# A hybrid decoder step on one core: where the refills, the last sums and the fourth quad's weights stand in the down products

## The reference

```
x = x + 0.5 * swiglu(rmsnorm(x, g_ffn1), w1_gate, w1_up, w1_down)
h = rmsnorm(x, g_mix) @ w_in          # RG-LRU heads | sliding-window attention heads
x = x + concat([lru_out, attn_out]) @ w_out
x = x + cross_attend(rmsnorm(x, g_xattn), memory keys, memory values)
x = x + 0.5 * swiglu(rmsnorm(x, g_ffn2), w2_gate, w2_up, w2_down)
y = rmsnorm(x, g_final)
swiglu(x) = (silu(x @ w_gate) * (x @ w_up)) @ w_down
```

## Time and profile before

| | |
|---|---|
| median of 3 runs | 2235.63 us (2232.41 to 2236.86) |
| the profiled execution's own time | 2234.07 us |
| its span | 2232.2 us |
| TensorE (PE) busy | 2128.1 us, 95% |
| VectorE (DVE) busy | 1595.1 us, 71% |
| ScalarE (ACT) busy | 772.9 us, 35% |
| GpSimd (POOL) busy | 514.1 us, 23% |
| DMA | 271.94 MB, 122 GB/s on average |

### The profile page before, as it was taken

One profiled execution on the slowest core, in us unless ns is written; L12 is line 12 of the kernel. 1 busy time (PEld: TensorE's weight loads), 2 busy tenths in 40 slices (PEclk: granted clock), 3 DMA queues, 4 the chain that ended last, 5 costly groups with the idle time before them and its releaser, 6 DMA issues. The chain is left out here.

```text
span 2232.2 us, 39480 instructions
## 1 busy us (share of the span) xinstructions
PE 2128.1 (95%) x15452; PEld 2013.8 (90%) x15452; DVE 1595.1 (71%) x2295; ACT 772.9 (35%) x1360; POOL 514.1 (23%) x499
## 2 busy tenths in 40 slices
PE   6899999999899999989999999998999999998998
PEld 5899999999898888877898887988999999998987
DVE  7877877878579578899526155368778778775884
ACT  6423323333233224557403034154233233322332
POOL 1011111101000256778635321520121121010002
PEclk9999999999999999999999999999999999999999
DMA  3223333255634121153411062312233233556332
GB/s 139 76 95 131 114 125 131 105 187 199 232 112 166 68 113 38 63 150 95 165 38 58 19 245 77 134 39 77 94 131 135 104 131 127 190 201 253 112 121 81
DMA packets 82296, 271.94 MB, mean 122 GB/s; under 512 B 9095, under 2 KB 21383, under 8 KB 68615
## 3 DMA queue, kind: packets, MB, share of 16 engines
q1 hardware_dynamic: 79232, 267.01, 32.6%
q10 hardware_dynamic: 2951, 3.35, 0.4%
HBM read 191.22 MB, written 76.32 MB: 120 GB/s over the span
## 5 line engine op out<-in xcount | busy, mean ns | idle before, releaser
L914 PE MATMUL ps<-act_hi,op_hi 128*128 128x272 f32 x1712 | 496.0, 290 | 31.2 <-DVE u L2321 22.7
L915 PE MATMUL ps<-act_lo,op_hi 128*128 128x272 f32 x1712 | 496.3, 290 | 0.0
L916 PE MATMUL ps<-act_hi,op_lo 128*128 128x272 f32 x1712 | 495.6, 289 | 0.0
L914 PE MATMUL ps<-t_hi,op_hi 128*128 128x272 f32 x1392 | 403.5, 290 | 7.3 <-DVE op_lo L2148 7.1
L916 PE MATMUL ps<-t_hi,op_lo 128*128 128x272 f32 x1392 | 403.0, 290 | 0.0
L915 PE MATMUL ps<-t_lo,op_hi 128*128 128x272 f32 x1392 | 402.8, 289 | 0.0
L914 PEld LDWEIGHTS ps<-act_hi,op_hi 128*128 128x128 f32 x1712 | 325.4, 190 | 34.5 <-issue 32.6
L1599 ACT ACTIVATE op_hi<-sums 128x512 fp32r<-128x512 f32 (+2 forms) x232 | 138.9, 599 | 548.9 <-DVE sums L2154 330.7
L822 POOL TENSOR_TENSOR hid_o<-hid_o 128x544 f32<-128x544 f32 x72 | 113.9, 1582 | 921.0 <-DMA hid<-hid_o 916.8
L915 PEld LDWEIGHTS ps<-act_lo,op_hi 128*128 128x128 f32 x1712 | 324.9, 190 | 0.0
L916 PEld LDWEIGHTS ps<-act_hi,op_lo 128*128 128x128 f32 x1712 | 324.5, 190 | 0.0
(11 more groups left out here) (354 smaller groups left out, 3952.1 us busy)
## 6 DMA issues: line engine op xcount, KB each, us to landing
raw_gu<-in_w_gu SPq DMA_DIRECT2D x40, 1024.0 KB, 6.8
w_raw<-in_w_plain SPq DMA_DIRECT2D x54, 512.0 KB, 3.3
hid<-hid_o SPq DMA_DIRECT2D x20, 1088.0 KB, 4.9
hid_t<-hid_o SPq DMA_DIRECT2D x18, 1088.0 KB, 4.0
hid_h<-sum_hi SPq DMA_DIRECT2D x16, 544.0 KB, 5.2
x<-x_keep SPq DMA_DIRECT2D x16, 544.0 KB, 6.2
raw_dq<-in_w_dq SPq DMA_DIRECT2D x8, 1024.0 KB, 7.8
ck_T<-in_ck SPq DMA_DIRECT2D x8, 1024.0 KB, 6.7
```

Of the source, the lines that this page charges most:

```text
L914: pe.matmul(out, wh, ah, start=(first and n == 0), stop=False, skip_group_check=goes_on)
L915: pe.matmul(out, wh, al, start=False, stop=False, skip_group_check=goes_on)
L916: ins = pe.matmul(out, wl, ah, start=False, stop=end, skip_group_check=goes_on)
```

## The change

Four edits. (1) SPLIT_OPS is (3, 4): operand 5 is stored raw, one high-part tile and one store less for each pair, and it is refilled on ACT and DVE like operand 6. (2) In a quad that opens a group, ACT makes the high parts of operands 5 and 6 after steps 1 and 2, and the next quad's weight parts 0 to 2 behind them; DVE makes the low part of operand 5 after C11, and the sums for the next quad after the low part of operand 6 instead of at the quad's start. (3) On SP, operand 6 of group 0 goes out ahead of the second row of x. (4) On SP, the weights of quad QUADS + 3 go out right behind those of QUADS + 2, ahead of the store of the last sums.

```diff
--- before.py
+++ after.py
@@ -82,10 +82,10 @@
 LAST_K = [2 * p + i for p in LAST_PAIRS for i in range(2)]
 LAST_ROWS = (2, 3, 6, 7)
 assert sorted([p for p0, kh in DOWN_GROUPS for p in range(p0, p0 + kh)] + [PAIR_AT.index(p) for p in LAST_PAIRS]) == list(range(FI))
-SPLIT_OPS = (3, 4, 5)
-RAW_OPS = (0, 1, 2, 6)
+SPLIT_OPS = (3, 4)
+RAW_OPS = (0, 1, 2, 5, 6)
 SUMMED = FI - 2
-OUTS = 3
+OUTS = 2
 SWAPS = 4
 QK = GRP + 1
 HALF_HEADS = NH // 2
@@ -250,11 +250,8 @@
         u3 = at("u3", [P, 2, TQ], X0 + KH * ROW + 2 * ROW)
         tmp = at("tmp", [P, 2, 2, TQ], X0 + KH * ROW + 2 * ROW + 4 * TH)
         hid_o = at("hid_o", [P, 2, T], X0)
-        sum_off = (X0 + 2 * ROW, X0 + KH * ROW + 3 * ROW + 4 * TH)
-        sum_hi = [at(f"sum_hi{i}", [P, 1, w], sum_off[i], F32R) for i, w in enumerate((T, TH))]
-        assert X0 + KH * ROW + 2 * ROW + 4 * TH + ROW <= sum_off[1] and sum_off[1] + 4 * TH <= A0
-        end_off = (X0 + KH * ROW + 2 * ROW + 4 * TH, X0 + KH * ROW + 2 * ROW)
-        end_hi = [at(f"end_hi{i}", [P, 1, w], end_off[i], F32R) for i, w in enumerate((T, TH))]
+        sum_hi = at("sum_hi", [P, 1, T], X0 + 2 * ROW, F32R)
+        end_hi = at("end_hi", [P, 1, T], X0 + KH * ROW + 2 * ROW + 4 * TH, F32R)
 
         def half(row, h):
             return row[:, h * TH:(h + 1) * TH].rearrange("p (a n) -> p a n", a=2)
@@ -450,7 +447,7 @@
                        hid_f=2 * NC + 4 * (FI - 1), hid_out=16 * (FI + 1), xg=KT, t_sum=8, t_hi=8, t_lo=8,
                        w_sum=4 * ALL_QUADS, w_hi=STEPS * ALL_QUADS, w_lo=STEPS * ALL_QUADS, quad_mm=STEPS * ALL_QUADS,
                        quad_ev=EVICTS * ALL_QUADS, p1_kept=ALL_QUADS, scaled=3 * QUADS // 2, up_own=3 * QUADS // 2,
-                       sum_hi=2 * SUMMED, sum_lo=2 * SUMMED, t_made=4 * SUMMED, t_out=16 * OUTS * SUMMED, x_added=3 * DOWN_QUADS,
+                       sum_hi=SUMMED, sum_lo=SUMMED, t_made=4 * SUMMED, t_out=16 * OUTS * SUMMED, x_added=3 * DOWN_QUADS,
                        mv_hi=len(RAW_OPS) * len(DOWN_GROUPS), mv_lo=len(RAW_OPS) * len(DOWN_GROUPS),
                        last_in=16 * (4 + 2 * NC), last_hi=4 + NC, last_lo=4 + NC, dn_mm=NC * KT, dn_ev=NC * KT)
         MV_IN = [sum(32 if j in SPLIT_OPS else 16 for j in range(i, STEPS, 3)) for i in range(3)]
@@ -596,9 +593,8 @@
                              hid_o[:, :, :].rearrange("p m n -> p (m n)")).then_inc(f["t_out"], 16)
 
             def store_highs(f, i, high=sum_hi):
-                sp.dma_start(t_in["hid_h"][:, i, 0:2, :].rearrange("p a n -> p (a n)"), high[0][:, 0, :].bitcast(F32))\
+                sp.dma_start(t_in["hid_h"][:, i, :, :].rearrange("p a n -> p (a n)"), high[:, 0, :].bitcast(F32))\
                   .then_inc(f["t_out"], 16)
-                sp.dma_start(t_in["hid_h"][:, i, 2, :], high[1][:, 0, :].bitcast(F32)).then_inc(f["t_out"], 16)
 
             def store_hidden(f, i, v):
                 sp.wait_ge(f["hid_f"], v)
@@ -624,7 +620,7 @@
                     store_hidden(f, i, i * 4 + upto(f, "hid_f", 2 * NC))
                     sp.wait_ge(f["w_lo"], i * (2 * STEPS) + upto(f, "w_lo", STEPS))
                     load_quad(f, w, i * 2 + 4, 0)
-                    store_sums(f, i, i * 2 + upto(f, "sum_lo", 0))
+                    store_sums(f, i, i + upto(f, "sum_lo", 0))
                     store_highs(f, i)
                 sp.wait_ge(f["w_lo"], upto(f, "w_lo", SUMMED * (2 * STEPS)))
                 load_quad(f, w, SUMMED * 2 + 3, 1)
@@ -640,23 +636,23 @@
                 sp.wait_ge(f["t_out"], upto(f, "t_out", 16 * OUTS * (SUMMED - 1)))
                 x_again(1, 0)
                 load_down(f, dq, QUADS + 1)
-                load_moving(f, 0, range(6))
-                sp.wait_ge(f["quad_mm"], upto(f, "quad_mm", STEPS * QUADS))
+                load_moving(f, 0)
                 sp.wait_ge(*x_back_again(f, 1, 1))
                 x_again(1, 1)
-                load_moving(f, 0, range(6, 7))
                 store_hidden(f, PAIR_AT.index(FI - 1), upto(f, "hid_f", 2 * NC + 4 * (FI - 1)))
                 for m in range(2):
                     x_again(2, m)
                 load_down(f, dq, QUADS + 2)
-                store_sums(f, PAIR_AT.index(FI - 1), upto(f, "sum_lo", 2 * SUMMED))
+                load_down(f, dq, QUADS + 3)
+                store_sums(f, PAIR_AT.index(FI - 1), upto(f, "sum_lo", SUMMED))
                 store_highs(f, PAIR_AT.index(FI - 1), end_hi)
                 sp.wait_ge(f["t_out"], upto(f, "t_out", 16 * OUTS * SUMMED))
                 for q in (3, 0):
                     for m in range(2):
                         x_again(q, m)
                 for n in range(QUADS + 3, ALL_QUADS):
-                    load_down(f, dq, n)
+                    if n > QUADS + 3:
+                        load_down(f, dq, n)
                     u = Quad(n - 2)
                     if u.ends_before_group():
                         load_moving(f, u.group() + 1)
@@ -1611,8 +1607,7 @@
 
                 made = 4 * SUMMED if u.down() else 0
                 act.wait_ge(f["t_made"], upto(f, "t_made", made) if made else u.turn(4, upto(f, "t_made", 0)))
-                act.activation(high[0][:, :, :], hid_o[:, 0:1, :], ACT.Copy).then_inc(f["sum_hi"], 1)
-                act.activation(high[1][:, :, :], hid_o[:, 1:2, 0:TH], ACT.Copy).then_inc(f["sum_hi"], 1)
+                act.activation(high[:, :, :], hid_o[:, 0:1, :], ACT.Copy).then_inc(f["sum_hi"], 1)
 
             def keep_p1(f, u):
                 act.wait_ge(f["quad_mm"], u.count(STEPS, upto(f, "quad_mm", 1)))
@@ -1636,8 +1631,8 @@
                     act.wait_ge(f["quad_mm"], u.count(STEPS, upto(f, "quad_mm", j + 1)))
                     if j == 0 and u.later():
                         keep_p1(f, u)
-                    if u.opens_group() and j == 3:
-                        refill_hi(f, u.group(), 6)
+                    if u.opens_group() and j in (1, 2):
+                        refill_hi(f, u.group(), 4 + j)
                     if u.opens_down() and j == 0:
                         quad_hi(f, u, s, STEPS - 1)
                     gate = s == 0 and not u.down()
@@ -1645,7 +1640,10 @@
                         quad_silu(f, u, 0)
                     if gate and j >= 5:
                         quad_silu(f, u, j - 4)
-                    if prepare and not (n.opens_down() and j == STEPS - 1):
+                    if u.opens_group() and j == 2:
+                        for v in range(3):
+                            quad_hi(f, n, 1 - s, v)
+                    elif prepare and not (u.opens_group() and j < 2) and not (n.opens_down() and j == STEPS - 1):
                         quad_hi(f, n, 1 - s, j)
                     if gate and j == 4 and u.i is not None:
                         sums_hi(f, u)
@@ -2266,11 +2264,10 @@
 
             def sums_lo(f, u, high=sum_hi):
 
-                for i, part in enumerate((hid_o[:, 0:1, :], hid_o[:, 1:2, 0:TH])):
-                    made = 2 * (SUMMED - 1) + i + 1 if u.down() else 0
-                    dve.wait_ge(f["sum_hi"], upto(f, "sum_hi", made) if made else u.turn(2, upto(f, "sum_hi", i - 1)))
-                    dve.tensor_tensor(part.bitcast(F32R), part, high[i][:, :, :].bitcast(F32), ALU.subtract)\
-                       .then_inc(f["sum_lo"], 1)
+                dve.wait_ge(f["sum_hi"], upto(f, "sum_hi", SUMMED) if u.down() else u.turn(1, upto(f, "sum_hi", 0)))
+                part = hid_o[:, 0:1, :]
+                dve.tensor_tensor(part.bitcast(F32R), part, high[:, :, :].bitcast(F32), ALU.subtract)\
+                   .then_inc(f["sum_lo"], 1)
 
             def refill_lo(f, g, j):
                 hi, lo, raw = operand(j, DOWN_GROUPS[g][1])
@@ -2321,13 +2318,10 @@
                     return dve.scalar_tensor_tensor(out=to[:, :, :], in0=ps[:, 2:4, 0:TQ], scalar=0.5, in1=p1[:, :, :],
                                                     op0=ALU.mult, op1=ALU.add).then_inc(f["quad_ev"], 1)
 
-                def last_low():
+                if not u.opens_down():
                     quad_lo(f, u, s, 6)
-                    if prepare:
-                        quad_sums(f, n, 1 - s)
-
-                if not u.opens_down():
-                    last_low()
+                if not u.opens_group() and prepare:
+                    quad_sums(f, n, 1 - s)
                 made(1)
                 dve.wait_ge(f["p1_kept"], u.count(1, upto(f, "p1_kept", 1)))
                 dve.wait_ge(f["quad_ev"], u.count(EVICTS, upto(f, "quad_ev", 0)))
@@ -2343,7 +2337,9 @@
                 made(2)
                 add_bank(0, 0, 0)
                 if u.opens_down():
-                    last_low()
+                    quad_lo(f, u, s, 6)
+                if u.opens_group():
+                    refill_lo(f, g, 5)
                 if not u.opens_group():
                     low(1)
                 if final:
```

## The result

| | kernel before | changed kernel |
|---|---|---|
| median | 2236.24 us (2232.41 to 2237.94, 4 runs) | 2203.31 us (2202.47 to 2212.15, 4 runs) |
| ratio | | 0.9864, interval 0.9836 to 0.9892 |
| profiled execution, span | 2234.07, 2232.2 | 2212.15, 2210.3 |
| TensorE, DVE busy | 2128.1, 1595.1 | 2127.8, 1593.4 |
| DMA | 271.94 MB | 261.91 MB |

The account below looks back on a forecast made before the run. TensorE, busy nearly throughout, was taken as the bound, with waits chiefly from a late-issued weight load. Terms 21.8 + 3.8 - 0.4 + 2.8 = 28.0 us took 2234.07 to 2206.1; median forecast 2208 us, range 2203 to 2212.

Parts of the forecast that it names:

- The load: Fourth down quad's weights, issued earlier, end TensorE's long waits and the low clock behind them: 21.8 us over both layers.
- rival E: Fourth down quad: the weight load isn't earlier, since the low copies hold it; 2235 us, chance 0.02.
- x as the next wait: First layer: x rows behind the last sums' store land at 569.1, delaying eviction C22; 0.5 us lost, nothing in the second.
- Rival B: First layer: x rows land 4 us or more later than taken and become the new wait; 2216 us, chance 0.07.
- Group 0: Down group 0's opening: operand 6 lands 4.2 us earlier, DVE's chain to p1 becomes 1.9 us earlier; 3.8 us, two layers.
- Step 5 waits for operand 5: Sign of being wrong: TensorE's step 5 waits for operand 5, where only 0.2 to 0.3 us was expected lost.
- The GpSimd term: Group 0's opening: GpSimd's four hidden-pair sums make four DVE instructions 1.15 us longer each, 4.6 us, unchanged by the edits.
- Locking: DVE and GpSimd's shared ports lock per instruction: four DVE instructions slowed; if all six, 2 x 1.15 us more a layer.
- rival C: Group openings gain in full, 6 us a layer, as weight sums slip ahead or GpSimd's come later; 2200 us, chance 0.11.
- rival A: Clock falls again where group 0 opens, after several short waits, 3.4 us per fall; 2215 us, chance 0.15.
- Groups 1 and 2: Later down groups: group 1 -0.4 us over both layers; group 2 1.4 us each from earlier QUADS+10 weights, 2.8 together.
- The loop: Quad loop: nine times one ACT copy, DVE copy and 272 KB store less, TensorE without gap; value 0, bounds 0 and 1.

Follow-up runs that it names:

- load_only: Kernel before with only the fourth down quad's weight load issued ahead of the store of the last sums; 2212.29 us, ratio 0.9894.
- three_split: Changed kernel's orders with operand 5 still stored split, so three operands split as before; 2211.78 us, ratio 0.9894 to the kernel before.
- x_swapped: Changed kernel with the x rows of q=0 issued ahead of those of q=3; 2210.3 us, ratio 0.9888 to the kernel before.
- after_again: Changed kernel unchanged, run and profiled a second time; 2205.31 us, ratio 0.9868 to the kernel before.
- pool_late: Changed kernel with GpSimd's last four hidden-pair sums held until p1 of quad QUADS+1 is kept; 2199.28 us, ratio 0.9842 to the kernel before.
- after_w10: Changed kernel with the weights of QUADS + 10 issued ahead of the last operands; 2205.53 us, ratio 0.9876 to the kernel before.
- sums_early: Changed kernel with the next quad's two weight sums back at the start of a group's opening quad; 2204.17 us, ratio 0.9859 to the kernel before.
- rest_only: Changed kernel without the moved weight load, which again stands behind the store of the last sums; 2224.04 us, ratio 0.9953 to the kernel before.
- before_again: Kernel before, unchanged, profiled a second time; 2237.53 us, span 2234.7.
- sums_pool: Changed kernel with the edits of both sums_early and pool_late; 2197.05 us, ratio 0.9832 to the kernel before.
- best_w10: sums_pool with the weights of QUADS + 10 issued ahead of the last operands; 2194.96 us, ratio 0.9831 to the kernel before.

## Why the prediction was right, step by step

**The load.** Right in cause and size, along the chain of the earlier trace rows. The terms were 21.8 us; edit (4) alone gave 21.7 by the medians, and 11.0 and 9.7 in the two group-0 stretches (12.2 and 9.6 forecast; the 1.7 us at C22, put at 0.5, are the difference in the first). The waits fell to nothing and the two low-clock stretches behind them went (rival E is out). The first term was read from one profile: the second profile of before has 9.2 us in that place and not 10.7.

**x as the next wait.** Rightly named, mis-sized in the end on the safe side. x was put at 569.1 with 0.5 us lost; it came at 564.90 with none. The four loads went out 2.8 us earlier than before (559.57), as the 1.3 us of the shorter store and group 0's shift give, and DVE had its row 5.3 us after that. With a third store in front the time was 7.8 us (load_only, 562.64 to 570.44) and 7.1 (three_split). In the seven profiles with two stores and the same order of x rows and weights it is 5.3 to 6.6, five of them below 6. So the third store goes with 0.5 to 2.5 us; by what means no run shows. In layer 2 it is 5.1 to 5.4 with three stores or two. Rival B's condition never came, and x_swapped shows what it costs near its edge. DVE stood 3.08 and 3.89 us at x; TensorE, whose idle stretch the sign of being wrong must mean (DVE's own was forecast), did not wait there.

**Group 0.** The landings were forecast at 516.2 and 519.0 and came at 517.0 and 519.7, DVE's low copy of operand 6 at 522.66 for 522.1. TensorE then waited 1.2 us for operand 5, not 0.2 to 0.3: DVE was waiting for ACT's t_hi, which waited for the transfer, so 0.8 us of landing went straight into that wait. "Step 5 waits for operand 5" was one of the prediction's signs of being wrong, and in this one opening it came. It was one late landing: in after_again the same copy started at 516.0 and the wait was 0.2, as forecast, and in layer 2 neither profile has one. Counted from the first refill, p1 was 1.4 us sooner than before in this opening and 2.3 to 2.7 in the other three, where 1.9 was claimed. The GpSimd term held: four DVE instructions at 1.74 to 1.84 us, the fifth at 0.68, and pool_late priced it at 3.9 to 4.3 us a layer. Locking was the better count than sharing: the number is GpSimd's four. The Trainium skill (SBUF — State Buffer, "SBUF: two separate sides") has it so for instructions with two SBUF inputs; the eviction of U2 in pool_late, with one of its inputs in PSUM, took 0.71 us beside GpSimd and agrees. That rival C's 8 us could be had was right too, but it took an edit: pool_late.

**The clock (rival A).** In layer 1 the fall did come, in both profiles (0.93 over 520:545; before had 0.86); in layer 2 the clock stayed up (1.00 over 1960:1990, 205 matmuls) where before it had been 0.83 over 1970:1990. What failed of A is its price. The fall stands ahead of p1, and there DVE's chain sets the pace and not TensorE. after_w10 has the same code and no fall in this opening:

```profile
520.00:545.00 25.00, 22.34 (x160) 21.56 (x159) 24.12 (x30) 8.68 (x14) 7.80 (x4) 0.93 0.35 134
...
520.00:545.00 25.00, 20.84 (x161) 20.05 (x160) 24.12 (x30) 8.65 (x14) 7.79 (x4) 1.00 0.35 136
```

The first row is after_again's, the second after_w10's. p1 is kept at 536.64 and 536.59, and group 0 takes 89.48 and 89.46 us. Without the fall TensorE only waits longer for p1, 1.5 us; with it, not at all. In layer 2 it is the other way round, after_w10 with the fall and the changed kernel without: 89.21 against 89.17 and 89.18. So a fall under this chain costs nothing, where A had put 3.4 us; in sums_early, behind p1, it does cost. Whether the clock falls is less settled. The Trainium skill (TensorE: Matmul & The Clock Gate, "A second HAM failure mode: psum-queue depth-cycling") holds that pauses, when frequent enough, make it swing. Ten openings here have the same wait of 1.9 us among shorter ones (after, after_again, rest_only, x_swapped, after_w10); five show the fall and five don't. What decides between them no run shows.

**Groups 1 and 2.** The cost of the moved sums in group 1 was put too low. Where the sums stand at the quad's start it takes 69.13 to 69.16 us, in nine of twelve openings of before, before_again, load_only, sums_early, sums_pool and best_w10; where they were moved, 69.81 to 69.84 in all fourteen. The moved sums thus cost 0.7 us in each layer, 1.3 together, where 0 and 0.4 had been claimed; TensorE waits 0.4 to 0.5 us for p1 there. The first profile of before hides it in layer 1, because operand 6 came late in it (a wait of 1.7 us, 1.1 in the second), and the 71.47 of before_again turns it into a gain in layer 2. Group 2's 1.4 us came in layer 1 (DVE's wait 3.21 to 0.69). The step that failed is its second half: in layer 2 the gain of the means is 0.5 and not 1.4, and against the first profile of before it is a loss of 0.3 to 0.7. DVE's wait and SP's last issues there:

```profile
2115.46 0.43 DVE L2137 TENSOR_TENSOR sums<-raw_dq 128x256 f32<-128x256 f32 x1 [2.52 <-DMA raw_dq<-in_w_dq]
...
2099.73 6.48 SPq L587 DMA_DIRECT2D act_raw<-hid  x6
```

In layer 1 the same six issues took 4.06 us. The queue moved more slowly in this layer's group 2, so the weights landed 32.8 us after the group's first refill (2115.46 - 2082.65; 32.5 in after_again), no sooner than the 32.2 of before's layer 2. Layer 1 had 31.0, and so had rest_only's layer 2, with the same code there. The 544 KB were saved; the pace at which the rest drained took it back in some executions.

**The loop.** Its value of 0 holds: layer 1's first refill goes out at 487.36 and 487.20 us in the two profiles of before, at 487.36 and 487.40 in the changed kernel's.

**The total.** 28.4 us by the ruler, 33 and 29 by the medians. The stretch between the down parts was 4.9 us longer in the two profiled executions of the changed kernel, and their own times (2212.15 and 2212.01) lie 6 to 10 us above its other executions. The nine profiles of the other variants have 1206.2 to 1211.0 there. Summed over stretches of ten microseconds with a clock below 0.95, this part misses 14 and 15 us of full clock in the two profiles of the changed kernel, 8 and 11 in before's, 8.5 in that of after_w10, where it took 1207.5 us. Part of it has a place. In the changed kernel:

```profile
1060.00:1070.00 10.00, 9.73 (x43) 8.55 (x45) 0.21 (x1) 1.02 (x1) 9.45 (x14) 0.50 0.15 54
```

and in after_w10, the same work:

```profile
1058.00:1068.00 10.00, 8.93 (x58) 6.88 (x58) 1.09 (x1) 2.11 (x3) 9.53 (x13) 1.00 0.27 78
```

One has the clock at its lower level for ten microseconds, the other not. In 1050:1060 ahead of it TensorE was busy 7.91 us in the one, with DVE and GpSimd busy nearly throughout, and 8.72 us in 1048:1058 of the other. Before's first profile has it (1077:1087, clock 0.52), its second doesn't. So the profiled execution came out 6 us above the 2206.1 worked out for it, while the medians of 2203.3 and 2205.3 lie 3 to 5 us below the 2208. Why both profiled executions of the changed kernel lie above its others is open; that of after_w10 (span 2200.5) doesn't.

That the sum came out within half a microsecond of 28.0 is partly luck. The load's terms hold by an experiment of their own. Of the others, group 0 gave more than was claimed, group 1 cost more, and half of group 2 didn't come; and the two means of layer 2 lean on before_again, whose groups 1 and 2 were 2.3 and 1.9 us longer than the first profile's. What the profiles bear out is 26 to 31 us, and the rest of the program moves by more than the small terms.

## What to carry to other kernels

A long wait that ends in a DMA is first a question of what stands ahead of its issue: one load moved past a store that waits gave three quarters of this gain. Before counting the gain, find the next transfer behind the same landing and its slack, by position in the waiting engine's order. Price a slow stretch only where the slowed engine sets the pace: the same fall of the clock cost nothing ahead of p1 and, as estimated for sums_early, 1.7 us behind it. And look at which engine's work runs beside a chain: moving four idle-time GpSimd instructions by 10 us was worth 4 us a layer, more than reordering the chain itself.

## What the hardware showed that was not expected

- A 128x512 DVE sum or copy takes 0.68 us alone and 1.73 to 1.86 beside GpSimd's 128x544 instructions (one in pool_late, met late, 1.22). Four GpSimd instructions slow four of DVE's, wherever the four are put; the eviction of U2, with an input in PSUM, stays at 0.71.
- With the same waits of TensorE, one of 1.9 us and some shorter ones, the granted clock fell in five openings of ten. Ahead of p1 the fall changed group 0's length by 0.04 us at most (89.48 against 89.46, 89.21 against 89.17).
- The same transfers let the weights of QUADS + 10 land 1.8 us later in one layer than in the other (32.8 and 31.0 us behind the group's first refill), and in the middle of the program the clock's low stretches changed place between two executions of one kernel (in before again 970:980 and 1370:1380 were low, in before they weren't), at 0.5 us of difference in that stretch's length.
